# Three of four gated one-hot rows made by POOL in one instruction per token, the rest by the vector engine from an iota in PSUM

## Time and profile before

| what | value |
|---|---|
| median of 3 runs | 1974.28 us (1973.35 to 1976.63) |
| span of the profiled execution, first to last instruction | 1971.0 us |
| busy in the span: PE, PEld, DVE, ACT, POOL | 1601.5, 1454.7, 1155.0, 832.3, 522.2 us |
| the chain that ended last: PE, DVE, issue, ACT | 54%, 15%, 5%, 3% |
| stage of the gate weights, first comparison to the last one's start | 1103.0 to 1219.1 us |
| expert loop, from its first matmul | 1227.8 us on |

### The profile page before, as it was taken

How to read it: one execution, slowest core, us unless ns; L and a number is a source line. 1 busy time by engine, 2 the same in 40 slices (tenths; PEclk the granted TensorE clock), 3 DMA queues, 4 the chain that set the end, 5 groups by cost and what they waited for, 6 DMA issues and landing times.

```text
span 1971.0 us, 28539 instructions
## 1 busy us (share of the span) xinstructions
PE 1601.5 (81%) x10659; PEld 1454.7 (74%) x10659; DVE 1155.0 (59%) x2079; ACT 832.3 (42%) x1374; POOL 522.2 (26%) x182
## 2 busy tenths in 40 slices
PE   7877887758867767888760465999999999999997
PEld 6876777747666766887760355999999999999996
DVE  3985246956654573322289998555555555555554
ACT  3334333336623344332320477444444444444443
POOL 6660546460043352663520364000000000000000
PEclk9878988969978888888885799999999999999998
DMA  8430225230022222342300001555555555555553
GB/s 336 150 129 1 89 83 171 86 128 1 1 86 86 86 86 86 129 139 93 111 1 0 0 0 64 174 189 192 178 184 192 182 181 191 187 177 189 191 177 111
DMA packets 32475, 238.28 MB, mean 121 GB/s; under 512 B 3600, under 2 KB 3728, under 8 KB 3984
## 3 DMA queue, kind: packets, MB, share of 16 engines
q1 hardware_dynamic: 32400, 237.27, 34.6%
HBM read 236.21 MB, written 1.05 MB: 120 GB/s over the span
## 4 chain that ended last, share of the span: by engine, by line
PE 54%; DVE 15%; issue 5%; ACT 3%; POOL 1%; DVEq 0%; DMA 0%; ACTq 0%; POOLq 0%
PE bank L764 18%; PE bank L498 12%; PE bank L531 6%; PE bank L534 6%; PE bank L501 6%; DVE raw L1513 3%; PE bank L590 2%; DVE hThi L1149 2%; PE bank L572 1%; DVE arena L1145 1%; DVE arena L1218 1%; DVE arena L1410 1%; ACT arena L898 1%; ACT whi L855 1%; DVE arena L1462 1%
## 5 line engine op out<-in xcount | busy, mean ns | idle before, releaser
L498 PE MATMUL bank<-hThi,whi 128*128 128x256 f32 x1024 | 251.0, 283 | 6.1 <-ACT whi L1046 6.1
L801 POOL TENSOR_TENSOR wlo<-arena,whi 128x2048 fp32r<-128x2048 f32 x44 | 205.7, 4679 | 180.9 <-ACT whi L855 180.9
L498 PE MATMUL bank<-hTlo,whi 128*128 128x256 f32 x1024 | 251.2, 283 | 0.0
L801 POOL TENSOR_TENSOR wlo<-raw,whi 128x2048 fp32r<-128x2048 f32 x44 | 207.2, 4712 | 123.8 <-ACT whi L855 123.8
L498 PEld LDWEIGHTS bank<-hThi,whi 128*128 128x128 f32 x1024 | 195.5, 191 | 11.4 <-issue 6.2
L764 PE MATMUL bank<-whi,ghi 128*128 128x512 f32 x512 | 202.9, 396 | 0.4 <-DVE glo L1535 0.3
L764 PE MATMUL bank<-whi,glo 128*128 128x512 f32 x512 | 202.9, 396 | 0.0
L764 PE MATMUL bank<-wlo,ghi 128*128 128x512 f32 x512 | 201.9, 394 | 0.0
L498 PEld LDWEIGHTS bank<-hTlo,whi 128*128 128x128 f32 x1024 | 195.8, 191 | 5.2
L1530 DVE TENSOR_TENSOR gact<-gact,arena 128x256 f32<-128x256 f32 x128 | 54.5, 426 | 236.6 <-ACT gact L1049 236.6
L1049 ACT ACTIVATE gact<-bank 128x256 f32<-128x256 f32 x128 | 49.4, 386 | 328.6 <-PE bank L501 328.6
(11 more groups left out here) (201 smaller groups left out, 3329.4 us busy)
## 6 DMA issues: line engine op xcount, KB each, us to landing
raw<-ex_in SPq DMA_DIRECT2D x86, 1024.0 KB, 4.9
raw<-w_in SPq DMA_DIRECT2D x44, 1024.0 KB, 4.9
arena<-w_in SPq DMA_DIRECT2D x44, 1024.0 KB, 4.9
xw<-ex_in SPq DMA_DIRECT2D x42, 1024.0 KB, 4.9
arena<-frt_in SPq DMA_DIRECT2D x1, 3904.0 KB, 26.2
arena<-tab_in SPq DMA_DIRECT2D x1, 1089.0 KB, 16.0
xw<-x_in SPq DMA_DIRECT2D x1, 1024.0 KB, 4.9
arena<-mem_in SPq DMA_DIRECT2D x1, 1024.0 KB, 4.7
```

Source lines behind the costliest of these rows:

```text
L498: mm(out, lhs, rhs, start=(k == 0), stop=False)
L801: G.tensor_tensor(wlo[:, u % 2, :], slots[u % RING], whi[:, u % 2, :], ALU.subtract).then_inc(lo_ready, 1)
```

## The change

POOL no longer multiplies rows that DVE made. It makes the three rows of A itself, each with one tensor_scalar of 128 x 128: the iota compared with the pointer `i1`, the result multiplied by the pointer `gate`. It needs only the transposed indices and a free ring slot, and its 192 instructions are written out without a loop. DVE copies the iota once into the first 128 columns of PSUM bank 4. Per group it makes the fourth row of A, gate included, with one tensor_scalar of 128 x 128 that has two pointers, and all of B as before; both read the iota from PSUM. ACT has no gate rows any more. The semaphores `hotG` and `hot_ready` are gone, and PE waits for `hotA` and `hotB`.

```diff
--- before.py
+++ after.py
@@ -160,7 +160,7 @@
         ftlo_pool, ftlo_dve = sem("ftlo_pool"), sem("ftlo_dve")
         uhi_ready, ulo_ready, vhi_ready, vlo_ready, ghi_ready, glo_ready = (
             sem(n) for n in ("uhi_ready", "ulo_ready", "vhi_ready", "vlo_ready", "ghi_ready", "glo_ready"))
-        hotA, hotG, hotB, x_kept = sem("hotA"), sem("hotG"), sem("hotB"), sem("x_kept")
+        hotA, hotB, iota_ready, x_kept = sem("hotA"), sem("hotB"), sem("iota_ready"), sem("x_kept")
         ex_loaded = [sem(f"ex_loaded{i}") for i in range(XRING)]
 
         proj_done, takenA, takenV = sem("proj_done"), sem("takenA"), sem("takenV")
@@ -183,7 +183,7 @@
             sem(n) for n in ("lam_a", "lam_v", "xc_ready", "ri_done", "ri_exp", "u_ready", "t_ready", "y_ready"))
         bias_ready = sem("bias_ready")
         sc_done, top_ready, g_exp = sem("sc_done"), sem("top_ready"), sem("g_exp")
-        hot_ready, wt_done, wt_taken = sem("hot_ready"), sem("wt_done"), sem("wt_taken")
+        wt_done, wt_taken = sem("wt_done"), sem("wt_taken")
         a_done, a_gelu, g_ready, v_done = sem("a_done"), sem("a_gelu"), sem("g_ready"), sem("v_done")
         out_ready, out_stored = sem("out_ready"), sem("out_stored")
         vchain, achain = sem("vchain"), sem("achain")
@@ -310,7 +310,8 @@
         la = R[:, 5152:6176].rearrange("p (b t) -> p b t", b=4)
         lb = R[:, 6176:7200].rearrange("p (b t) -> p b t", b=4)
 
-        iota4 = tb("iota", KEEP, keep).unsqueeze(1).to_broadcast([P, 4, P])
+        iota = tb("iota", KEEP, keep)
+        iota_ps = bank[4][:, 0:P]
         QP = R[:, 0:4096].rearrange("p (b t) -> p b t", b=16)
         SCR = R[:, 4096:8192].rearrange("p (t b n) -> p t b n", t=TT, b=16)
         subk = QT.rearrange("p b t -> p (b t)").rearrange("p (b n) -> p b n", b=16)
@@ -739,7 +740,6 @@
             with pe.Fori(0, T // 16) as g:
                 for r in range(4):
                     pe.wait_ge(hotA, g * 4 + (r + 1))
-                    pe.wait_ge(hotG, g * 4 + (r + 1))
                     pe.wait_ge(hotB, g * 4 + (r + 1))
                     pe.wait_ge(wt_taken, g * 4 + (r + 7))
                     for j in range(4):
@@ -801,19 +801,15 @@
                 G.tensor_tensor(wlo[:, u % 2, :], slots[u % RING], whi[:, u % 2, :], ALU.subtract).then_inc(lo_ready, 1)
 
 
-            def gate_rows(r, gate):
-                G.tensor_tensor(onehot[:, r, 0, 0:3], onehot[:, r, 0, 0:3], gate.unsqueeze(2).to_broadcast([P, 3, P]),
-                                ALU.mult).then_inc(hotA, 1)
-
-            gates = idxT[:, 2, :].rearrange("p (g r j) -> p r g j", r=4, j=4)
             pool.wait_ge(tr_taken, tr_all("sel1"))
-            for r in range(4):
-                pool.wait_ge(hot_ready, r + 1)
-                gate_rows(r, gates[:, r, 0, 0:3])
-            with pool.Fori(1, T // 16) as g:
-                for r in range(4):
-                    pool.wait_ge(hot_ready, g * 4 + (r + 1))
-                    gate_rows(r, gates[:, r, bass.ds(g, 1), 0:3].rearrange("p g j -> p (g j)"))
+            for n in range(T // 4):
+                if n >= 4:
+                    pool.wait_ge(wt_done, n - 3)
+                for j in range(3):
+                    tok = 4 * n + j
+                    last = G.tensor_scalar(onehot[:, n % 4, 0, j, :], iota, idxT[:, 0, tok:tok + 1],
+                                           idxT[:, 2, tok:tok + 1], ALU.is_equal, ALU.mult)
+                last.then_inc(hotA, 1)
 
 
         @block.scalar
@@ -1015,26 +1011,14 @@
                 A(E, E, ACT.Exp).then_inc(g_exp, 1)
 
             W4 = arena[:, :].rearrange("p (n g r t) -> p r g t n", g=T // 16, r=4, t=4)
-            gates = idxT[:, 2, :].rearrange("p (g r j) -> p r g j", r=4, j=4)
-            act.wait_ge(tr_taken, tr_all("sel1"))
-
-            def gate_row(r, gate):
-                A(onehot[:, r, 0, 3, :], onehot[:, r, 0, 3, :], ACT.Copy, scale=gate).then_inc(hotG, 1)
-
             def w_out(r, to):
                 A(to, bank[6 + r % 2][:, :].rearrange("p (t n) -> p t n", t=4), ACT.Copy).then_inc(wt_taken, 1)
 
-
-            for r in range(4):
-                act.wait_ge(hot_ready, r + 1)
-                gate_row(r, gates[:, r, 0, 3:4])
-                if r > 0:
-                    act.wait_ge(wt_done, r)
-                    w_out(r - 1, W4[:, r - 1, 0])
+            for r in range(1, 4):
+                act.wait_ge(wt_done, r)
+                w_out(r - 1, W4[:, r - 1, 0])
             with act.Fori(1, T // 16) as g:
                 for r in range(4):
-                    act.wait_ge(hot_ready, g * 4 + (r + 1))
-                    gate_row(r, gates[:, r, bass.ds(g, 1), 3:4].rearrange("p g j -> p (g j)"))
                     act.wait_ge(wt_done, g * 4 + r)
                     before = W4[:, (r - 1) % 4]
                     w_out((r - 1) % 4, before[:, bass.ds(g - (1 if r == 0 else 0), 1)].rearrange("p g t n -> p (g t) n"))
@@ -1508,19 +1492,23 @@
                     take_transposed("sel0")
             take_transposed("sel1")
 
-            def hot_rows(r, i1, i2):
-                for s, index, ready in ((0, i1, hot_ready), (1, i2, hotB)):
-                    V.tensor_tensor(onehot[:, r, s], iota4, index.unsqueeze(2).to_broadcast([P, 4, P]),
-                                    ALU.is_equal).then_inc(ready, 1)
+            V.tensor_copy(iota_ps, iota).then_inc(iota_ready, 1)
+
+            def hot_rows(r, i1, gate, i2):
+                V.tensor_scalar(onehot[:, r, 0, 3, :], iota_ps, i1, gate, ALU.is_equal, ALU.mult)
+                V.tensor_tensor(onehot[:, r, 1], iota_ps.unsqueeze(1).to_broadcast([P, 4, P]),
+                                i2.unsqueeze(2).to_broadcast([P, 4, P]), ALU.is_equal).then_inc(hotB, 1)
 
             idx4 = idxT.rearrange("p s (g r j) -> p s r g j", r=4, j=4)
             dve.wait_ge(lo_ready, 2 * NCHUNK)
+            dve.wait_ge(iota_ready, 1)
             for r in range(4):
-                hot_rows(r, idx4[:, 0, r, 0], idx4[:, 1, r, 0])
+                hot_rows(r, idx4[:, 0, r, 0, 3:4], idx4[:, 2, r, 0, 3:4], idx4[:, 1, r, 0])
             with dve.Fori(1, T // 16) as g:
                 for r in range(4):
                     dve.wait_ge(wt_done, g * 4 + (r - 3))
-                    hot_rows(r, *(idx4[:, s, r, bass.ds(g, 1)].rearrange("p g j -> p (g j)") for s in range(2)))
+                    i1, gate = (idx4[:, s, r, bass.ds(g, 1), 3:4].rearrange("p g j -> p (g j)") for s in (0, 2))
+                    hot_rows(r, i1, gate, idx4[:, 1, r, bass.ds(g, 1)].rearrange("p g j -> p (g j)"))
 
 
             Wg = arena[:, :]
```

## The result

The changed kernel takes **2005.8 us** (median of 4 runs, 2004.6 to 2006.4) against 1974.8 us of the kernel before (4 runs, 1973.4 to 1976.6): ratio 1.0154, 95% interval 1.0140 to 1.0169. It is slower by 31 us, where 1948 us was forecast, in a range that ended at 1986.

A forecast was written before the change was run, and what follows sets the result against it. The gate-weight stage was bound by vector-engine comparisons standing still while POOL worked, 1.835 us a group. POOL's 1.40 would save 27.4 us, less 1.4 (half clock), plus 0.6 (first group): 26.6, from 1974.3 to 1948 us, range 1933 to 1986.

The forecast's parts named there:

- part 5: POOL's three 128-element instructions per group: 0.45 us each, 1.40 us a group with wait and signal, setting the pace.
- The lower bound (0.31) and the upper (1.11): POOL's new instruction: at least the fixed part and half the slope, at most the whole present 384-element multiplication, in us.
- What bounds the kernel before: Gate-weight stage: 1.835 us a group, two vector-engine comparisons (1.22) plus some 0.61 us standing still while POOL worked.
- Parts 1 and 2: Vector engine: 512-element comparison 0.61 us start to start, short two-pointer row 0.26 + 0.06; together 0.93 us a group.
- Parts 3 and 4: ScalarE keeps one copy of 1.06 us a group; TensorE's eight passes take 1.15 at full clock, 1.67 for the first four.
- the term for the half clock: Start of the stage: TensorE paces at 1.67 instead of 1.40 us for about five groups, giving back 1.4 us.
- 0.05 us for wait and signal: POOL, per group: an allowance on top of 1.35 us for its three instructions, making 1.40 us.
- The other sign of being wrong: POOL: a stall at its first such instruction or in its 192 unrolled ones, where code is brought in; no size given.
- Rival A: POOL quick, 0.31 to 0.40 us an instruction, so TensorE paces at some 1.20 a group: 1936 us, chance 0.25.
- Rival B: POOL's pointers cost a fixed part, 0.63 us an instruction, worse bound than the vector engine was: 1980 us, chance 0.15.
- Rival C: POOL's comparison as dear as the present 384-element instruction, 1.11 us: 97 us lost, 2071 us, chance 0.05.
- Rival D: Vector engine and POOL still exclude each other, times adding to 2.33 us a group: 2005 us, chance 0.03.

The follow-up runs named there:

- psum_only: Kernel before, with both vector-engine comparisons reading the iota from PSUM; POOL and ScalarE multiply the gates as before: 1945.9 us, ratio 0.9855.
- psum_pool4: Kernel before, with both comparisons reading the iota from PSUM and POOL multiplying all four rows, ScalarE only copying: 1937.7 us, ratio 0.9811.
- psum_first_only: Kernel before, with only the first of the two vector-engine comparisons reading the iota from PSUM, the second from SBUF: 1946.1 us, ratio 0.9852.
- pool_mult_mult: Changed kernel, with POOL's two operations both multiplications by the same two pointers, the comparison left out: 1939.9 us.
- split_2_2: Changed kernel, with two rows per group made by POOL instead of three, and two by the vector engine: 1955.3 us, ratio 0.9905.
- index_in_sbuf: Changed kernel, with the vector engine's 512-element comparison reading the iota from SBUF again, its short one still from PSUM: 2021.3 us, ratio 1.0253.

## Why the prediction was wrong

The step that failed is part 5, **POOL's instruction at 0.45 us**. It measures 0.774. The working laid a line through POOL's two-input rows, 2.105 ns an element over 0.18 us, and argued that one tensor input fewer would lower it; in fact the one-input instruction has 3.35 ns and 0.34 us. Half of the miss of 0.32 us is the fixed part (0.16), half the elements ((3.35 - 2.105) x 128 = 0.16). The lower bound (0.31) and the upper (1.11) did hold it, but the range was drawn by the value near the lower one. By this step alone the sum turns: 63 x (1.835 - 2.32) = -30.6 us instead of +27.4. A line through the quicker two-input rows of psum_only and psum_pool4 (1.69 ns) would have made the forecast still more hopeful; a line through another operation said nothing of this one.

Part by part:
- **What bounds the kernel before** was right. The 0.61 us of standing still is confirmed by psum_only, where the comparisons lose it and the pace falls by 0.49 to 1.34. What was missing there: POOL's 1.11 us also held a wait, 0.28 us, and psum_first_only shows it.
- **Parts 1 and 2** were right: 0.68 us for every comparison in the changed kernel, and 0.41 us for the short row's form with a second pointer (0.34 + 0.06 had been said). The rest of the vector engine's pace is idle time.
- **Parts 3 and 4** were right and of no account, since both engines wait. The clock at 0.72 was not foreseen. At the true pace of 2.32 the term for the half clock is gone too: TensorE's 2.07 us for a group there (1.67 from start to start) is under POOL's.
- The **0.05 us for wait and signal** was nothing: POOL finds wt_done of four groups before long there. The other sign of being wrong, a stall at the first or within the 192 unrolled instructions, didn't come either: POOL has no idle time among them, and unrolled in the same way pool_mult_mult steps at 0.428.
- **Rival A** had the Trainium skill's best case beside it ("GPSIMD Engine Reference", section 3.1, 1.8 cycles an element for a tight loop). This tensor_scalar takes 3.35 ns, which at the 1.2 GHz of the Trainium skill is 4.0 cycles; only the pair of multiplications, at 0.84 ns or 1.0 cycle, is quicker than that best case.
- **Rival B** named what happened, POOL a worse bound than the vector engine had been, with its point of decision at 0.595 us; split in three, the fixed parts are paid three times. Its price (0.63) was too low, and its reason half right: the pointers are a small part of it, the fixed part and the rate the large ones. Section 7 of the Trainium skill's "GPSIMD Engine Reference", small read commands of 102 cycles, made 0.62 of it; with both pointers taken out 0.065 us of the step went, against the 0.17 that it would have been (0.16 if the durations are compared, so that these two runs don't settle it).
- **Rival C** (1.11) was too dear.
- **Rival D** gave 2005 us and a pace of 2.33, next to the measured 2005.8 and 2.32, by luck: it had POOL at 0.45 us and the vector engine's 0.93 added to it as waiting. The comparisons are at 0.68 us, POOL's steps are the same with and without an instruction of the vector engine beside them, and in split_2_2, where the vector engine has more rows, the step stays at 0.773. What such waiting looks like, index_in_sbuf shows.
- The chances were wrong in size: 0.15 for B with a form that no row showed, against a threshold of 0.595 that lay in the middle of bounds of 0.31 and 1.11, was too little.

## What to carry to other kernels

Two changes had been tied together. One, the operand moved to PSUM, ends a stall that stands in no wait view and is worth 1.45% alone; the other, moving work onto POOL in small instructions, cost more than all of it. Look for an instruction with two durations in turns, ask what the neighbouring engine does during the longer one, and change the operand before moving the work. An engine's price for an operation that it has not run in the kernel is not to be had from its other operations: where a change hangs on one, measure that form first, and put the chance by where the threshold lies between the bounds.

## What the runs showed of the hardware that was not expected

- POOL's tensor_scalar on float32: 0.34 us and 3.35 ns an element for compare and multiply with two pointers, 0.58 us at 128 elements for one operation of either kind, but 0.428 us for two multiplications, at 0.84 ns an element. Why that pair is quicker than a single multiplication stays open.
- POOL's tensor_tensor with a broadcast input: 0.826 us at 384 elements and 1.042 at 512 when nothing is in its way, 1.11 beside a comparison with two SBUF inputs.
- The exclusion goes both ways and isn't for the whole of every instruction. "SBUF — State Buffer", section "Who interferes with whom", of the Trainium skill calls the port pair that the vector engine and GpSimd share an exclusive lock, which a vector instruction with two SBUF inputs contends for as well; of the vector engine's two-port modes it says that whoever issues first has the pair for the whole instruction and the other is blocked. For POOL's tensor_tensor of 2048 elements agree: an instruction of 0.29 us took 4.65. For its tensor_scalar of 128 elements the trace doesn't agree: in index_in_sbuf POOL, which started first, held up a comparison only until 0.30 us after its start, of 0.79, and a comparison that came 0.10 to 0.12 us behind it ran at its usual 0.68 us while POOL's instruction took 0.5 us more.
